# A six-stage float32 block on one core: opening loads, rotary adds, row maxima and scan order changed

## The reference

```python
sc = einsum(q, k) * scale                  # q, k rotated, 4 heads x 2 maps
p = softmax(where(chunk_causal_mask(i, s), sc, -inf))
w = p[:, :, 0] - lam * p[:, :, 1]
o = rmsnorm(einsum(w, v), subln) * (1 - lam_init)
u = g[..., :C] * sigmoid(g[..., C:]);  y = conv31(u) + b;  silu(layernorm(y))
```

```python
h_t = a * h_(t-1) + B u_t    (complex);   y = Re(C h) + d * u;   gelu(y), glu
cq, ckv = rmsnorm(x Wq'), rmsnorm(x Wkv');  softmax(q k^T + mask) v  for 6 heads
```

## Time and profile before

| | |
|---|---|
| median of 3 runs | 1943.38 us |
| lowest, highest | 1943.25, 1949.54 us |
| the profiled execution, its own time | 1944.46 us |
| its span, first to last instruction | 1942.7 us |
| mean granted clock of TensorE | 0.961 of full |
| busy: PE, DVE, ACT, POOL | 92%, 49%, 39%, 48% |

### The profile page before, as it was taken

One profiled execution on the slowest core, in us unless ns is written; L12 is line 12 of the kernel. 1 busy time (PEld: TensorE's weight loads), 2 busy tenths in 40 slices (PEclk: granted clock), 3 DMA queues, 4 the chain that ended last, 5 costly groups with the idle time before them and its releaser, 6 DMA issues.

```text
span 1942.7 us, 20117 instructions
## 1 busy us (share of the span) xinstructions
PE 1779.1 (92%) x7496; PEld 1341.6 (69%) x7496; DVE 954.9 (49%) x1444; ACT 749.4 (39%) x1234; POOL 937.9 (48%) x1100
## 2 busy tenths in 40 slices
PE   8999989989988988789999999987878899999996
PEld 6776557678766755466888888764445678888885
DVE  2043436766836997636514323447567453033244
ACT  4264564365454224734332222432232442322231
POOL 4433125458943441134656556576124346565562
PEclk9999999999999999789999999998778999999998
DMA  5222112222112221012333333211001213323331
GB/s 188 87 65 66 33 44 85 66 65 87 55 33 76 76 76 33 23 54 88 98 98 98 98 98 98 76 55 33 11 11 33 66 59 98 98 94 97 98 98 65
DMA packets 39553, 139.90 MB, mean 72 GB/s; under 512 B 4512, under 2 KB 4640, under 8 KB 39328
## 3 DMA queue, kind: packets, MB, share of 16 engines
q1 hardware_dynamic: 39456, 138.61, 22.2%
HBM read 136.50 MB, written 2.10 MB: 71 GB/s over the span
## 4 chain that ended last, share of the span: by engine, by line
PE 75%; DVE 16%; ACT 6%; issue 2%; POOL 1%; DMA 1%; SPq 0%; DVEq 0%; ACTq 0%
PE ps L623 18%; PE ps L624 17%; PE ps L625 17%; DVE ps L1850 4%; PE ps L683 2%; PE ps L640 1%; PE ps L646 1%; PE ps L637 1%; PE ps L1247 1%; PE ps L660 1%; PE ps L662 1%; PE ps L661 1%; DVE arena L761 1%; PE ps L928 1%; DVE x L764 1%
## 5 line engine op out<-in xcount | busy, mean ns | idle before, releaser
L2777 POOL TENSOR_TENSOR wl<-raw,wh 128x256 fp32r<-128x256 f32 x988 | 811.2, 853 | 895.5 <-ACT wh L710 895.3
L710 ACT ACTIVATE wh<-raw 128x1024 fp32r<-128x1024 f32 x247 | 260.9, 1057 | 562.4 <-PE ps L625 499.3
L623 PE MATMUL ps<-hh,wh 128*128 128x512 f32 x1068 | 438.7, 411 | 22.0 <-POOL wl L2777 5.2
L624 PE MATMUL ps<-hl,wh 128*128 128x512 f32 x1068 | 420.4, 394 | 0.0
L625 PE MATMUL ps<-hh,wl 128*128 128x512 f32 x1068 | 420.4, 394 | 0.0
L623 PE MATMUL ps<-mh,wh 128*128 128x512 f32 x632 | 261.9, 414 | 27.8 <-DVE nrm L2458 7.2
L623 PEld LDWEIGHTS ps<-hh,wh 128*128 128x128 f32 x1068 | 203.2, 190 | 80.0 <-issue 16.6
L624 PE MATMUL ps<-ml,wh 128*128 128x512 f32 x632 | 250.8, 397 | 0.0
L625 PE MATMUL ps<-mh,wl 128*128 128x512 f32 x632 | 250.4, 396 | 0.0
L624 PEld LDWEIGHTS ps<-hl,wh 128*128 128x128 f32 x1068 | 203.5, 191 | 45.8 <-issue 6.0
L625 PEld LDWEIGHTS ps<-hh,wl 128*128 128x128 f32 x1068 | 203.2, 190 | 43.7
(11 more groups left out here) (476 smaller groups left out, 2451.9 us busy)
## 6 DMA issues: line engine op xcount, KB each, us to landing
raw<-in_w SPq DMA_DIRECT2D x247, 512.0 KB, 3.4
x<-in_x SPq DMA_DIRECT2D x8, 256.0 KB, 7.9
out<-x SPq DMA_DIRECT2D x8, 256.0 KB, 2.0
arena<-in_rope SPq DMA_DIRECT2D x3, 512.0 KB, 5.7
arena<-in_dec SPq DMA_DIRECT2D x1, 1024.0 KB, 11.1
mats<-in_mats SPq DMA_DIRECT2D x1, 576.0 KB, 7.6
arena<-in_lw SPq DMA_DIRECT2D x1, 512.0 KB, 3.4
arena<-in_levels SPq DMA_DIRECT2D x1, 448.0 KB, 4.1
```

What stands on the lines that cost most here:

```text
L623: e.matmul(ps[b][:], a, xh, start=first, stop=False)
L624: e.matmul(ps[b][:], a, xl, start=False, stop=False)
L710: e.activation(wh[:, n % NHL, :], raw[:, n % NRAW, :], ACT.Copy).then_inc(rounded.sem, rounded.up(n))
L2777: e.tensor_tensor(wl[:, n % NHL, cut(i, 2)], raw[:, n % NRAW, cut(i, 2)], wh[:, n % NHL, cut(i, 2)].bitcast(F32), SUB).then_inc(split.sem, ...
```

## The change

In the opening of `even`: SP loads slot 0 in two halves with a semaphore for the first, the order of x, slots and `mats` is another, and slots 3 to 5 go ahead of rope1 and dec; ACT rounds slot 0 by halves and slots 1 and 2 at `hi` 2 and 4, copies EXACT at `rs` and rounds slots 3 and 4 there; PE and POOL wait for a half of slot 0; one warming matmul less. In `diff`: `ub` 0 is evicted first, ahead of `lb`; the adds of the rotation (L1827) go from DVE to POOL, and who waited for DVE waits for POOL; `v1` 0 stands ahead of `ln` 0; the remainder of the gate is a step of its own (`fn` 4), one j behind; half of the second set of rows is merged with `fn`, the other half with `p`. In `ssm`: the square of ckv is a step `ns` ahead of the second latent's norm; `nq` 1 and `nk` 1 go ahead of evictions; a new `close` puts `qb` behind `qa` and `r2` n + 1 behind `r2` n, ahead of the scan's items; s3c is dropped, and `s4` adds its two parts in PSUM with twice as many products; the scaled identity is made by ACT; gelu has one operation less; s4 6 and `z1` 1 go ahead of what was merged around them.

```diff
     u = [group(("ua", j), 8, ("e", ("ua", j))) + group(("ub", j), 8, ("e", ("ub", j)), ("um", j)) for j in range(4)]
-    out = opening(*OPENS["diff"]) + [("lb",), ("e", ("ua", 0)), ("e", ("ub", 0)), ("um", 0), ("e", ("ua", 1)), ("tb",)]
+    out = opening(*OPENS["diff"]) + [("e", ("ub", 0)), ("lb",), ("e", ("ua", 0)), ("um", 0), ("e", ("ua", 1)), ("tb",)]
...
     out += merge(qk[0], conv[78:94]) + merge(merge(qk[1], rows[0]), conv[94:])
-    norm = [("ln", n) for n in range(3)] + [("fn", n, j) for n in range(4) for j in range(4)]
+    norm = [("ln", n) for n in range(3)]
+    act = [("fn", n, j) for n in range(3) for j in range(4)]
+    act += [("fn", 3, 0), ("fn", 3, 1), ("fn", 4, 0), ("fn", 3, 2), ("fn", 4, 1), ("fn", 3, 3), ("fn", 4, 2), ("fn", 4, 3)]
...
     part = groups([("p", d) for d in range(KT)], 4, "pe")
-    out += merge(values[0] + rows[1], norm + part[:-12]) + values[1] + part[-12:] + [("v3", h) for h in range(4)]
+    out += merge(values[0], norm) + merge(rows[1][:16], act) + merge(rows[1][16:], part[:-12]) + values[1] + part[-12:]
+    out += [("v3", h) for h in range(4)]
...
+def close(steps, a, b, kinds=None):
+    i, j = steps.index(a) + 1, steps.index(b)
+    moved = [s for s in steps[i:j] if kinds is None or s[0] in kinds]
+    return steps[:i] + [s for s in steps[i:j] if s not in moved] + [b] + moved + steps[j + 1:]
...
     out = opening(*OPENS["ssm"]) + [("an", 0), ("e", c[0]), ("e", c[1])]
-    out += group(c[2], 8, ("e", c[2]), ("nq", 0), ("an", 1))
-    out += group(c[3], 8, ("e", c[3]), ("nq", 1), ("nk", 0), ("an", 2))
-    out += group(c[4], 8, ("e", c[4]), ("nk", 1), ("ka", 0))
+    out += group(c[2], 8, ("e", c[2]), ("nq", 0), ("ns", 0), ("an", 1))
+    out += group(c[3], 8, ("nq", 1), ("e", c[3]), ("nk", 0), ("an", 2))
+    out += group(c[4], 8, ("nk", 1), ("e", c[4]), ("ka", 0))
...
         scan += [("s1", i), ("s1b", i), ("s2", i), ("s2b", i), ("s1", i + 1), ("s1b", i + 1), ("s2c", i), ("s3", i), ("s3b", i)]
-        scan += [("s3c", i), ("s2", i + 1), ("s2b", i + 1), ("s2c", i + 1), ("s3", i + 1), ("s3b", i + 1), ("s3c", i + 1)]
+        scan += [("s2", i + 1), ("s2b", i + 1), ("s2c", i + 1), ("s3", i + 1), ("s3b", i + 1)]
...
             scan += [(n, i // 4) for n in ("z1", "z2", "z3", "z4")]
-    out += merge(mul, scan)
+    mul = merge(mul, scan)
+    kinds = {s[0] for s in scan}
+    for g in range(3):
+        mul = close(mul, ("qa", g), ("qb", g), kinds)
+    for n in range(0, 24, 2):
+        mul = close(mul, ("r2", n), ("r2", n + 1))
+    last = [s for s in scan[-4:]]
+    mul = [s for s in mul if s not in last]
+    at = mul.index(("s4", 6)) + 1
+    out += mul[:at] + last[:1] + merge(last[1:], mul[at:])
...
                     claim(e, bank(stage, g))
+                n, i = divmod(PLACE[stage, step], SLOT)
...
                 if (stage, step) in STARTS:
-                    e.wait_ge(rounded.sem, rounded[STARTS[stage, step]])
+                    e.wait_ge(rounded.sem, rounded[n] if n else rounded["half"])
+                elif n == 0 and i == SLOT // 2:
+                    e.wait_ge(rounded.sem, rounded[0])
...
+        HALF = 64 * SLOT
...
+            if n == 0:
+                e.wait_ge(s_first, 16)
+                e.activation(wh[:, 0, 0:HALF], raw[:, 0, 0:HALF], ACT.Copy).then_inc(rounded.sem, rounded.up("half"))
+                e.wait_ge(s_raw[0], 16)
+                e.activation(wh[:, 0, HALF:], raw[:, 0, HALF:], ACT.Copy).then_inc(rounded.sem, rounded.up(0))
+                return
...
             e.wait_ge(dve.sem, dve["warm"])
-            for n in range(7):
+            for n in range(6):
...
             for step in STEPS["even"]:
-                round_ahead(e, "even", step)
...
                 kind = step[0]
-                if kind == "hi" and 1 <= step[1] <= NHL:
-                    round_slot(e, step[1] - 1)
-                if step == ("hi", NHL + 1):
+                if kind != "w" or step[1] not in OPENS["even"]:
+                    round_ahead(e, "even", step)
+                if kind == "hi" and step[1] in (1, 2, 4):
+                    round_slot(e, step[1] // 2)
+                if kind == "rs":
...
                         e.activation(R(name), M(name), ACT.Copy).then_inc(consts.sem, consts.up(name))
+                    round_slot(e, NHL)
+                    round_slot(e, NHL + 1)
...
                     h, qt, w = unit(n)
-                    e.wait_ge(dve.sem, dve["rotated", ("dk", h)])
+                    e.wait_ge(s.pool.sem, s.pool["rotated", ("dk", h)])
...
                     e.tensor_tensor(q, ps[6][:], d_rope[:, 1, :], MUL).then_inc(dve.sem, dve.up("ra_sin", g))
-                    e.wait_ge(dve.sem, dve["ra_sin", g])
-                    e.tensor_tensor((dq4 if g[0] == "dq" else dk4)[:, g[1], :], q, r, ADD).then_inc(dve.sem, dve.up("rotated", g))
...
                         e.tensor_tensor(yj, yj, t, MUL).then_inc(dve.sem, dve.up("mix", 4 + j))
+                    elif n == 4:
...
                     if before:
-                        e.wait_ge(dve.sem, dve["rotated", before])
+                        e.wait_ge(pool.sem, pool["rotated", before])
...
                 e.wait_ge(s.act.sem, s.act["e", ("ub", j)])
+                e.wait_ge(s.dve.sem, s.dve["e", ("ua", j)])
...
                 e.tensor_tensor(du[:, j, CW:], du[:, j, CW:], d_gt[j % 2], MUL).then_inc(s.pool.sem, s.pool.up("um", j))
+            elif step[0] == "rb":
+                g = step[1]
+                _, q, r = rotating(g)
+                e.wait_ge(s.dve.sem, s.dve["ra_sin", g])
+                e.tensor_tensor((dq4 if g[0] == "dq" else dk4)[:, g[1], :], q, r, ADD).then_inc(s.pool.sem, s.pool.up("rotated", g))
...
                     claim(e, 4)
-                    e.wait_ge(dve.sem, dve["r3", n])
+                    e.wait_ge(act.sem, act["diagonal", n])
...
                         e.wait_ge(dve.sem, dve["cim"])
-                    e.wait_ge(dve.sem, dve["s_out", i + 1])
-                    for n in (i, i + 1):
-                        e.matmul(ps[5][rows32(n), :], cre[:, n, :], lane_of(n)[0], start=True, stop=False)
-                    for n in (i, i + 1):
-                        p = e.matmul(ps[5][rows32(n), :], cim[:, n, :], lane_of(n)[1], start=False, stop=True)
+                    e.wait_ge(dve.sem, dve["s_h", i + 1])
+                    for turned, c in enumerate((cre, cim, cim, cre)):
+                        for n in (i, i + 1):
+                            p = e.matmul(ps[5][rows32(n), :], c[:, n, :], lane_of(n)[turned], start=(turned == 0), stop=(turned == 3))
...
                     e.reciprocal(col[:, 1:2], col[:, 1:2]).then_inc(dve.sem, dve.up("over_sum", n))
-                    e.wait_ge(dve.sem, dve["over_sum", n])
-                    e.tensor_scalar(over_sum(n), M("ident"), col[:, 1:2], None, MUL).then_inc(dve.sem, dve.up("r3", n))
...
                     e.wait_ge(dve.sem, dve["s_f", i])
-                    e.tensor_tensor(w6, w6, sinT, MUL).then_inc(dve.sem, dve.up("s_g", i))
+                    e.scalar_tensor_tensor(out=w6, in0=w6, scalar=-1.0, in1=sinT, op0=MUL, op1=MUL).then_inc(dve.sem, dve.up("s_g", i))
...
                     e.tensor_tensor(w5, w5, sinT, MUL).then_inc(dve.sem, dve.up("s_h", i))
-                elif kind == "s3c":
-                    i = step[1]
-                    vre, vim, w5, w6 = lane_of(i)
-                    e.wait_ge(dve.sem, dve["s_g", i])
-                    e.tensor_tensor(vre, vre, w6, SUB).then_inc(dve.sem, dve.up("s_i", i))
-                    e.wait_ge(dve.sem, dve["s_h", i])
-                    e.tensor_tensor(vim, vim, w5, ADD).then_inc(dve.sem, dve.up("s_out", i))
...
                     e.wait_ge(dve.sem, dve.n)
-                    e.tensor_scalar(w5, w5, 0.044715, 1.0, MUL, ADD).then_inc(dve.sem, dve.up("z_inner", j))
+                    e.tensor_scalar(w5, w5, 0.044715 * 1.5957691216057308, 1.5957691216057308, MUL, ADD).then_inc(
+                        dve.sem, dve.up("z_inner", j))
...
                     e.wait_ge(dve.sem, dve.n)
-                    e.tensor_tensor(w5, w5, zj, MUL).then_inc(dve.sem, dve.up("z_cubic", j))
-                    e.wait_ge(dve.sem, dve.n)
-                    e.tensor_scalar(w5, w5, 1.5957691216057308, None, MUL).then_inc(dve.sem, dve.up("z1", j))
+                    e.tensor_tensor(w5, w5, zj, MUL).then_inc(dve.sem, dve.up("z1", j))
...
                         e.activation(mh[:, 6 + j, :], cq[:, j, :], ACT.Copy).then_inc(act.sem, act.up("latent", "q", j))
-                elif kind == "nk" and step[1] == 0:
+                elif kind == "ns":
...
                     e.activation(s_tmp[3], ckv, ACT.Square).then_inc(act.sem, act.up("ckv_square"))
-                elif kind == "nk":
+                elif kind == "nk" and step[1] == 1:
...
                                  accum_out=col[:, 1:2]).then_inc(act.sem, act.up("r2", n))
+                elif kind == "r3":
+                    n = step[1]
```

(28 more changed lines are left out.)

1 line of the change is left out of this document (added).

## The result

The changed kernel takes 1911.14 us (median of four runs, 1910.65 to 1917.43) against 1944.62 for the kernel before on the same chip, 33.5 us less; the ratio is 0.9824, with a 95% interval of 0.9808 to 0.9840. The profiled execution is the longest of the four, 1917.43 us around a span of 1915.6, so that its own difference to the profile of before is 27.

What follows compares the result with a forecast made beforehand. PE, busy 92% of the span, was taken to bound the kernel. Terms of -5.3 (even), -6 (diff) and -18.4 (ssm) sum to -29.7 us against 1944.46; forecast 1914 us, range 1897 to 1933.

Steps and rivals of the forecast that it cites:

- A: Opening of even: reordered loads and roundings and slot 0 in halves save 5.3 us, between 3.5 and 6.6.
- B: Opening of diff: evicting `ub` 0 first adds two table loads and delays `ub` 1, costing 1.3 us.
- C: Rotation of diff: moving eight adds from DVE to POOL saves 3.0 us.
- Rival 3: Rotation of diff: POOL's SBUF adds hold DVE, +4 instead of -3, total 1921 us; chance 0.06.
- Taps done before 760: Sign for the rotation of diff: DVE finishes the convolution's taps before 760 us.
- D: End of diff: `v1` 0 earlier and the gate's remainder split off save 4.4 us.
- Diff in all: Sum of the three diff terms, +1.3 - 3.0 - 4.4: 6 us saved, between 0 and 9.
- E: Ssm: fewer PE waits, less the cost of more `s4` products, save 18.4 us, between 8 and 24.
- Rival 1: Ssm mixer: PE's clock recovers with the waits, 12 to 15 us more saved, about 1901 us; chance 0.17.
- rival 2: Ssm gives most back: `s4` at lower clock, half of `r1` waits form again; total 1926 us; chance 0.16.
- rival 5: Ssm slower: ACT's queue with the diagonals holds the exponentials, total +8, 1951 us; chance 0.04.
- Rivals 4: Ssm orders do not matter: each wait removed opens the next; within 0.5%, 1938 us; chance 0.07.

Runs made afterwards that it cites:

- best_b: Changed kernel with scaled identity on DVE, lam step in two, gates over 20 row steps, slot 1 rounded ahead of `hi` 3; ratio 0.9805 to the kernel before.
- open_lam_kscan: Changed kernel with diff's old opening order (lam step ahead of evicting `ub` 0) and, in ssm, no joining of `qb` to `qa`; ratio 0.9883 to the kernel before.
- rotary_ckv: Changed kernel with diff's rotation add on DVE again and, in ssm, the square of ckv back behind the latent copies; ratio 0.9869 to the kernel before.
- diagonal_dve: Changed kernel with ssm's scaled identity on DVE again, right behind its reciprocal; ratio 0.9813 to the kernel before.

## Why the prediction was right, and where it was not

Forecast 1914.0, measured 1911.14, inside the range and faster by 1.8%, well beyond the 0.5% that a measurement can tell. The sum was -29.7 against -33.5, by terms of which two were too large and one too small. The way was not the forecast's: of the 33 us, half are a gain of clock that its sum put at nothing, and its waits fell short in diff and ssm. That the number was near is in part luck.

- **A** (-5.3): measured -3.8. The wait for slot 3 went as said. The start of 1.4 was right: 2.3 in the pair, but from 7.81 to 8.52 us in the four profiles with the old opening to 6.18 to 6.95 in the ten with the new, 1.5 by their means. At `rs` 4.9 us are won. What I had not looked for are new waits of PE for ACT at `hi` 1 and 2, 1.1 to 1.9 us together in nine profiles, up to 0.5 with the old opening; best_b, which rounds slot 1 behind `hi` 2, has 0.43 there and reaches `rs` at 32.66. And 1.1 us is lost between `rs` and the end of the stage, as busy time. (The 32.5 us given as the sign for `rs` do not follow from A: 38.77 - 5.3 is 33.5.)
- **B** (+1.3): two further loads of 1.28 as said, `ub` 1 late by 1.4; at the stage's end +0.7.
- **C** (-3.0): 3.0 in the changed kernel, though 0 without D. The taps kept their mean, in this group of DVE (count, busy us, mean ns, idle before):

```profile
L1882 DVE SCALAR_TENSOR_TENSOR ps<-arena,vec,ps 128x512 f32<-128x512 f32 x116 | 87.4, 753 | 3.0
```

  753 ns as in the earlier trace rows, with eight adds of POOL among them. Rival 3, by the rule of the Trainium skill (Perfetto Trace Analysis, Optimizing Scalar/DVE Operations), did not come; this case shows it only for taps whose accumulator is in PSUM. "Taps done before 760" was wrong: the last starts at 765.8, 161.7 us after the stage's start where it was 160.7. B's delay stands in it: without B (open_lam_kscan) it is 159.2, without C (rotary_ckv) 163.2. So the last tap comes only 1.5 us earlier for the 6.4 us of adds taken off DVE.
- **D** (-4.4): -2.6 by undoing, and nothing without C. The tiles of `p` came faster as said. "PE's queue shorter" left out ACT: its steps for the gates take as long as before, and PE's 4.26 for an identity and 3.02 for `p` became 5.59 for a copy.
- **Diff in all** (-6): -2.2. The single undoings sum to -4.9 and don't add, since C and D are worth something only together. The forecast priced waits alone, and idle time fell by 0.3 us (in five profiles of this code it is 39.1 to 40.4, of 40.7 and 39.8 in the two of the old); the rest is busy time. Which wait C and D share was not tried.
- **E** (-18.4): -27.1. Waits: -25.8 forecast (all terms but s4), -17.95 measured. ckv (4.5 of 5.0), s4 (6.9 of 7.4) and the diagonal (1.0) came as said, q_sin gave more (7.2 of 5.3). `r1` kept 12.6 instead of 9, and `r4` rose by 5.8, the term that the forecast did not have: its scaled identity stands in ACT's order, and diagonal_dve, with the identity on DVE, has 3.6 instead of 10.3. The -1.5 of the late z steps stands in no run alone. Clock: 0 forecast, -16.0 measured. Rival 1 put that at 12 to 15 and had a chance of 0.17; its clock came in full, and its total, 1901, did not, since 8 us of waits stayed. Of these, `r1`'s 3.6 are rival 2's kind and `r4`'s 5.8 are rival 5's. The term that the sum put at nothing, the clock, failed, and E was near because two errors of opposite sign met. The sign that it named for rival 1, a clock over 0.88, was set too high: 0.88 was already it.
- **The range**: 1897 does not follow from the bounds that it names. A, diff and half of E's favourable side are -6.6 - 9 - 21.2 = -36.8, 1908; the lower end rests on rival 1 alone.
- **Rivals 4 and 5**: against 4 stand the joinings, 11 us each when undone. 5 had its mechanism (ACT's order holds `r4`) but at 1.0 us of idle time.

## What to carry to other kernels

Cut a stage into PE's idle time and PE's busy time, before and after, and price both: in a stage where the granted clock is under 1, a wait removed can also raise the clock of the products behind it, here by nearly as much again (18.0 of waits, 16.0 of clock). It is no fixed rate: undoing a part cost from 0.1 us of busy time for 4.4 of idle (rotary_ckv) to 9.2 for 1.8 (open_lam_kscan). Join steps of one engine that become ready together; don't put a step ahead whose input another engine is still making. When an edit takes one wait away, look which wait on the same chain PE reaches next, and whether an earlier engine's order already holds it.

## What the runs showed that I had not expected

The granted clock can multiply small waits. Undoing the joining of qb added 1.8 us of idle time and 9.2 us of busy time; taking the maxima apart 4.6 and 6.9. The same code is uneven too: with the identity on DVE ssm had 33.7 to 35.0 us of idle time in three profiles and 228.4 to 235.1 of busy time, at a clock of 0.92 to 0.95, and the untouched odd took 276.4 to 281.3. What decides which of these a run gets stays open.
